# RWKV feature and scan stages: norms ahead of decays, key products on GpSimd, reciprocals right behind the masks

## Chip, cores and metric

The program runs on one core of a Trainium2 chip, in one launch. The metric is device microseconds of a whole execution, as the median of several runs.

## What is computed

One layer of a hybrid network. Its mixer has an RWKV-7 branch and an mLSTM branch, over 256 context tokens and then 512 latent tokens; a product-key expert block follows. The change touches the RWKV-7 branch alone:

```python
w_log = -softplus(-(w0 + einsum("btr,zrc->btzc", tanh(wd), w_up))) - 0.5
decay = exp(-exp(w_log))
a = sigmoid(a0 + einsum("btr,zrc->btzc", ad, a_up))
kk = k * k_k;  kk = kk / max(norm(kk, per head), 1e-12)
k_eff = k * (1 + (a - 1) * k_a)
# per head and direction, over time:
S = S * w_t - (S kk_t) (kk_t * a_t)^T + v_t k_t^T;   out_t = S r_t   # latent stream only
```

There are 8 heads of 64 channels and 2 directions (z = 0 and 1; z = 1 runs backwards in time). The context stream only hands its state on; the latent stream also gives outputs.

## The kernel before

Channels lie on partitions, tokens along the free dimension. 512 channels are 4 tiles of 128 (`PAIRS`, index c; two heads each). Phases follow each other, each a block of hand-written programs for the five engines that meet in semaphores; every engine runs its own list in order. The two touched phases run twice: `phase_rwkv_features` and `phase_rwkv_scan` for the context (tag `_c`, T = 256), then for the latents (tag `_x`, T = 512).

**Feature phase.** ScalarE takes `Tanh` of the decay input (L558), squares kk (L561) in one operation, and then goes through eight units n = (z, c). In each it takes the `Tanh` of the decay projection (`rw_th`, L567), an `Exp` into `w65` (L573, named w in the trace) and the `Tanh` of the rate projection into `qa` (L576). TensorE makes two projections a unit into four PSUM banks used in turn (L590, L592; a unit waits for the `qa` of the unit two before it), and behind all eight the four norm products of ones with the squares (L597), which take the same banks. VectorE scans each unit's decays into cumulative products `G` (L624; in the trace TENSOR_TENSOR_SCAN, in the listings below SCALAR_TENSOR_TENSOR), where the four scans of z = 1 wait until all eight `Exp` are there. It bounds the norms (L630); ScalarE takes `Ln` and `Exp` of them (L579, L581), each behind a table load; VectorE normalises `kk` (L633), and then makes, for each z over all four tiles: a = 0.5 tanh + 0.5 in `qa` (L637), the keys `ke` = k (1 - k_a + a k_a) in two steps (L639, L641) and the rates `qa` = a kk (L642). GpSimd does nothing here.

**Scan phase.** Chunks of `C` = 64 tokens, 4 for the context and 8 for the latents; two groups g, one a direction, in turn. GpSimd prepares a chunk (`prepare`): `pr` (kk by G, and r by G for the latents), then, once VectorE has `ginv` = 1/G (`inverse`, L957), `qs` = qa ginv and `ks` = ke ginv. TensorE multiplies `qs` and `ks` by `pr` (L880, marks Q and K): `pr` is `RW` = 3 C wide, its parts being the keys, the receptances (for the context a block of zeros), and a unit matrix. VectorE applies the masks to the products (`tm`, `td`, `bt`, `mt`, `at`), and five levels (`LEVELS`) of products and subtractions invert a triangular matrix (`ti`, `td` on VectorE, `xd` on ScalarE, the level masks `lm` on GpSimd, L757). Then R, U, O (latents) and S products, and VectorE updates the state `st` (L1001, L1003). The reciprocals for chunk i + 1 stand on VectorE behind the last level of chunk i, so `qs` and `ks` of chunk i + 1 come after that on GpSimd. TensorE starts a chunk's Q of group g when its `ks`, and the `st` of the chunk before, are done.

## Time and profile before

| | |
|---|---|
| median of 3 runs | 2789.89 us (2789.34 to 2801.12) |
| profiled execution | 2820.51 us, its span 2818.5 us |
| busy in the span: PE, DVE, ACT, POOL | 2583.1, 1331.7, 1026.9, 768.5 us |
| granted TensorE clock, mean | 0.94 |

The phases the change touches lie in this stretch of the same span, 458 us of it:

| stretch, us | what | PE busy | DVE | ACT | POOL | granted clock |
|---|---|---|---|---|---|---|
| 391.5 to 424.5 | context features | 12.89 | 18.93 | 16.34 | 0.00 | 0.55 |
| 424.5 to 546.5 | context scan, 4 chunks | 109.02 | 63.84 | 41.01 | 44.65 | 0.94 |
| 546.5 to 599.5 | latent features | 18.60 | 32.59 | 24.09 | 0.00 | 0.61 |
| 599.5 to 849.5 | latent scan, 8 chunks | 237.04 | 136.24 | 90.16 | 100.56 | 0.97 |

Phases meet in barriers, so a stretch ends when its last engine does. In a timeline row the columns are start, duration, engine, line and operation, output and inputs with shapes, count, and in brackets the idle time before it and who ended it. A row that merges several instructions gives the time from the first start to the last end. One fp32 matmul shows as two records.

### The profile page before, as it was taken

The numbers are of one execution on the slowest core, as the hardware profiler recorded it, in microseconds if no ns is written. First come the engines' busy times: TensorE is split into PE (matmuls) and PEld (weight loads), VectorE is DVE, ScalarE is ACT, GpSimd is POOL, SyncE is SP. The second block draws the span as 40 slices with busy tenths as digits, with TensorE's granted clock in tenths as the row PEclk, the third lists the DMA queues.
The fourth block names the chain that finished last, engine by engine and source line by source line (L and its number), as shares of the span: only waits on it lengthen the run. The fifth ranks groups of instructions, "written<-read, shape, count | busy, mean of one in ns | idle before, by whom it ended". The sixth has DMA issues, their size and how long they took to land. (4 is left out here: it accounts for less than half of the span.)

```text
span 2818.5 us, 53257 instructions
## 1 busy us (share of the span) xinstructions
PE 2583.1 (92%) x19772; PEld 2115.8 (75%) x19772; DVE 1331.7 (47%) x2679; ACT 1026.9 (36%) x1763; POOL 768.5 (27%) x627
## 2 busy tenths in 40 slices
PE   7999948849995898699999999999999999999998
PEld 3884527739993786588778888887888888888886
...
GB/s 251 192 149 37 0 0 2 2 1 0 0 1 95 89 97 52 121 127 69 122 122 173 216 174 170 168 194 216 145 134 220 192 195 189 198 187 200 184 203 60
DMA packets 163765, 348.58 MB, mean 124 GB/s; under 512 B 13352, under 2 KB 79400, under 8 KB 161648
## 3 DMA queue, kind: packets, MB, share of 16 engines
...
q8 instruction: 45, 0.74, 0.1%
...
## 5 line engine op out<-in xcount | busy, mean ns | idle before, releaser
L85 PE MATMUL ps_a<-h_hi,u_hi 128*128 128x512 f32 x1024 | 406.9, 397 | 14.1 <-issue 5.6
L2522 DVE TENSOR_TENSOR v_lo<-v_raw,v_hi 128x1024 fp32r<-128x1024 f32 x128 | 158.3, 1236 | 536.1 <-ACT v_hi L2480 536.1
L86 PE MATMUL ps_a<-h_hi,u_lo 128*128 128x512 f32 x1024 | 400.6, 391 | 0.0
L87 PE MATMUL ps_a<-h_lo,u_hi 128*128 128x512 f32 x1024 | 400.4, 391 | 0.0
L2480 ACT ACTIVATE v_hi<-v_raw 128x1024 fp32r<-128x1024 f32 x128 | 135.8, 1061 | 478.5 <-PE ps_a L87 470.2
L85 PE MATMUL ps_y<-gated_hi,v_hi 128*128 128x512 f32 x768 | 299.6, 390 | 3.1 <-DVE gated_lo L2524 3.1
L86 PE MATMUL ps_y<-gated_hi,v_lo 128*128 128x512 f32 x768 | 299.3, 390 | 0.0
L87 PE MATMUL ps_y<-gated_lo,v_hi 128*128 128x512 f32 x768 | 299.2, 390 | 0.0
L85 PEld LDWEIGHTS ps_a<-h_hi,u_hi 128*128 128x128 f32 x1024 | 193.8, 189 | 53.5 <-issue 14.2
L87 PEld LDWEIGHTS ps_a<-h_lo,u_hi 128*128 128x128 f32 x1024 | 193.3, 189 | 40.6
L86 PEld LDWEIGHTS ps_a<-h_hi,u_lo 128*128 128x128 f32 x1024 | 193.7, 189 | 37.9
L1876 ACT ACTIVATE act<-ps_a 128x512 f32<-128x512 f32 x128 | 76.4, 597 | 394.9 <-PE ps_a L87 383.8
L2332 POOL TENSOR_SCALAR mixed<-iota,w_token 128x128 f32<-128x128 f32 x128 | 149.5, 1168 | 213.3 <-PE ps_w L2351 197.7
L1860 POOL TENSOR_TENSOR u_lo<-u_raw,u_hi 128x1024 fp32r<-128x1024 f32 x64 | 155.5, 2434 | 175.4 <-ACT u_hi L1856 175.4
L1860 DVE TENSOR_TENSOR u_lo<-u_raw,u_hi 128x1024 fp32r<-128x1024 f32 x64 | 78.4, 1225 | 242.3 <-ACT u_hi L1856 242.3
L85 PEld LDWEIGHTS ps_y<-gated_hi,v_hi 128*128 128x128 f32 x768 | 144.6, 188 | 33.6 <-DVE v_lo L2522 3.5
L86 PEld LDWEIGHTS ps_y<-gated_hi,v_lo 128*128 128x128 f32 x768 | 144.6, 188 | 30.0
L87 PEld LDWEIGHTS ps_y<-gated_lo,v_hi 128*128 128x128 f32 x768 | 144.4, 188 | 30.1
L1856 ACT ACTIVATE u_hi<-u_raw 128x1024 fp32r<-128x1024 f32 x128 | 134.5, 1051 | 41.1 <-DMA u_raw<-in_uT 41.1
L1667 POOL TENSOR_TENSOR mg_w_lo<-mg_raw,mg_w_hi 128x1024 fp32r<-128x1024 f32 x36 | 87.7, 2436 | 197.8 <-ACT mg_w_hi L1716 197.8
L2383 ACT ACTIVATE w_block<-ps_w 128x512 f32 x128 | 141.3, 1104 | 0.0
L2351 PEld LDWEIGHTS ps_w<-mixed 128*128 128x128 f32 x1024 | 124.1, 191 | 5.0
...
## 6 DMA issues: line engine op xcount, KB each, us to landing
u_raw<-in_uT SPq DMA_DIRECT2D x128, 512.0 KB, 3.5
v_raw<-in_v SPq DMA_DIRECT2D x128, 512.0 KB, 4.8
a_scratch<-act SPq DMA_DIRECT2D x128, 256.0 KB, 2.2
w_scratch<-w_block SPq DMA_DIRECT2D x8, 4096.0 KB, 12.0
...
gated<-a_scratch SPq DMA_DIRECT2D x128, 256.0 KB, 4.8
...
```

The lines of the kernel that those rows point to most:

```text
L85: pe.matmul(out, wh, xh, start=first, stop=False)
L86: pe.matmul(out, wl, xh, start=False, stop=False)
L87: return pe.matmul(out, wh, xl, start=False, stop=last)
L1667: g.tensor_tensor(wl[:, k], raw[:, k], wh[:, k], ALU.subtract).then_inc(w_lo, 1)
L1856: act.activation(self.uh[:, q], self.raw[:, q % 2], ACT.Copy).then_inc(self.hi, 1)
L1860: eng.tensor_tensor(self.ul[:, q], self.raw[:, q % 2], self.uh[:, q], ALU.subtract).then_inc(self.lo, 1)
L1876: act.activation(self.act[:, q % 2], self.ps[q % 2][:], ACT.Gelu).then_inc(self.out, 1)
L2332: g_.tensor_scalar(oi[:, s, SUB - 1], iota, cur[:, s, 0:1], cur[:, s, 1:2], ALU.is_equal, ALU.mult).then_inc(built_p, 1)
L2351: m = pe.matmul(ps[s][:, k, :], oi[:, s, k], oj[:, s, k], start=True, stop=True)
L2383: act.activation(wb[:, half, :, bass.ds(g * BODY + dt, SUB)].rearrange("p j t -> p t j"), ps[s][:], ACT.Copy).then_inc(evac[s], 1)
L2480: act.activation(vh[:, q], v_raw[:, q], ACT.Copy).then_inc(v_hi, 1)
L2522: v.tensor_tensor(vl[:, q], v_raw[:, q], vh[:, q], ALU.subtract).then_inc(v_lo, 1)
```

## The change

In the feature phase the squares are made tile by tile ahead of the units; the norm products stand behind the second unit's projections and have PSUM banks of their own (`ps_rn`). ScalarE's order in a unit becomes decay `Tanh`, rate `Tanh`, `Exp`; its `Ln` and `Exp` for the norms stand between the units of z = 0 and z = 1. GpSimd makes the keys from tanh directly (a `tensor_scalar` and a `tensor_tensor` per unit). VectorE makes the rates with one `scalar_tensor_tensor` per unit, (tanh + 1) kk, which is twice the rate, and waits for the unit's `tensor_scalar` on GpSimd; the factor 0.5 goes into the masks and into `qt`. In the scan the context's `pr` loses its block of zeros (`RW` = 2 C), and the reciprocals for the next chunk stand right behind the masks. The diff leaves out unchanged parts and the two old loops over the units, on ScalarE and for the scans, which stand in the functions above.

```diff
@@ -520,12 +520,12 @@
             same = (r[:, None] // (2 * size)) == (r[None, :] // (2 * size))
             return same & ((r[:, None] // size) != (r[None, :] // size))
 
-        out[:, z, M_NEG1_ST] = -(off(1) & s_t).astype(np.float32)
+        out[:, z, M_NEG1_ST] = -0.5 * (off(1) & s_t).astype(np.float32)
         out[:, z, M_STRICT] = s_t
-        out[:, z, M_NEG_INCL] = -(s_t | np.eye(C, dtype=bool)).astype(np.float32)
+        out[:, z, M_NEG_INCL] = -0.5 * (s_t | np.eye(C, dtype=bool)).astype(np.float32)
         out[:, z, M_INCL] = s_t | np.eye(C, dtype=bool)
         for n, size in enumerate(LEVELS):
-            out[:, z, M_OFF + n] = off(size) & t_s
+            out[:, z, M_OFF + n] = 0.5 * (off(size) & t_s)
     return np.concatenate([out, out], 0)
 
@@ phase_rwkv_features @@
         half = sb("rw_half" + tag, [P, 4, PAIRS])
-        one_ka = sb("rw_1ka" + tag, [P, PAIRS])
+        ka = sb("rw_ka" + tag, [P, 2, PAIRS])
         w65 = sb("w65" + tag, [P, PAIRS, nch, C + 1])
         first = sb("w65_first" + tag, [P, nch, C + 1])
...
         ps = [ctx.enter_context(nc.psum_tensor(f"ps_rf{k}" + tag, [P, 512], F32)) for k in range(4)]
+        ps_n = [ctx.enter_context(nc.psum_tensor(f"ps_rn{k}" + tag, [P, 512], F32)) for k in range(PAIRS)]
...
         @block.scalar
         def _(act):
             act.activation(f[0:64, 12, :], f[0:64, 12, :], ACT.Tanh).then_inc(tanh_wd, 1)
+            for c in range(PAIRS):
+                act.wait_ge(sq_in, c + 1)
+                act.activation(tmp[:, c, :], b.kk[:, c, 0:T], ACT.Square).then_inc(sq_done, 1)
             act.wait_ge(half_done, 1)
-            act.wait_ge(sq_in, 1)
-            act.activation(tmp[:], b.kk[:, :, 0:T], ACT.Square).then_inc(sq_done, 1)
...
+            for n, (z, c) in enumerate(units):
+                act.wait_ge(proj, n + 1)
+                act.activation(th[:, n % 2], ps[2 * (n % 2)][:, 0:T], ACT.Tanh, bias=half[:, z, c:c + 1],
+                               scale=0.5).then_inc(th_done, 1)
+                act.activation(b.qa[:, z, c, 0:T], ps[2 * (n % 2) + 1][:, 0:T], ACT.Tanh,
+                               bias=half[:, 2 + z, c:c + 1], scale=0.5).then_inc(a_done, 1)
+                act.wait_ge(th_done, n + 1)
+                if z == 1:
+                    act.wait_ge(slot_done, 2)
+                act.activation(w65[:, c, :, 1:] if z == 0 else w65[:, c, :, 0:C],
+                               th[:, n % 2].rearrange("p (n t) -> p n t", t=C), ACT.Exp,
+                               bias=b.eps[:, 2:3], scale=-HALF_DECAY).then_inc(dec_done, 1)
+                if n == PAIRS - 1:
+                    act.wait_ge(norm_max, 1)
+                    act.activation(tmp[:], tmp[:], ACT.Ln).then_inc(norm_root, 1)
+                    act.wait_ge(norm_root, 1)
+                    act.activation(tmp[:], tmp[:], ACT.Exp, scale=-0.5).then_inc(norm_root, 1)
         @block.tensor
         def _(pe):
-            pe.wait_ge(tanh_wd, 1)
-            for n in range(2 * PAIRS):
-                z, c = n // PAIRS, n % PAIRS
+            def project(n):
+                z, c = units[n]
                 if n >= 2:
                     pe.wait_ge(a_done, n - 1)
                 pe.matmul(ps[2 * (n % 2)][:, 0:T], wa_up[0:64, z, c * P:(c + 1) * P], f[0:64, 12, :],
                           start=True, stop=True)
                 pe.matmul(ps[2 * (n % 2) + 1][:, 0:T], wa_up[64:P, z, c * P:(c + 1) * P], f[64:P, 12, :],
                           start=True, stop=True).then_inc(proj, 1)
-            pe.wait_ge(sq_done, 1)
-            pe.wait_ge(a_done, 2 * PAIRS)
+            pe.wait_ge(tanh_wd, 1)
+            for n in range(2):
+                project(n)
             for c in range(PAIRS):
-                mm = pe.matmul(ps[c][:, 0:T], b.block_ones[:], tmp[:, c, :], start=True, stop=True)
-            mm.then_inc(norm_mm, 1)
+                pe.wait_ge(sq_done, c + 1)
+                pe.matmul(ps_n[c][:, 0:T], b.block_ones[:], tmp[:, c, :], start=True, stop=True).then_inc(norm_mm, 1)
+            for n in range(2, len(units)):
+                project(n)
+        @block.gpsimd
+        def _(g):
+            g.wait_ge(half_done, 1)
+            for n, (z, c) in enumerate(units):
+                g.wait_ge(a_done, n + 1)
+                ke = b.ke[:, z, c, 0:T]
+                g.tensor_scalar(ke, b.qa[:, z, c, 0:T], ka[:, 0, c:c + 1], ka[:, 1, c:c + 1], ALU.mult,
+                                ALU.add).then_inc(pool, 1)
+                g.wait_ge(pool, 2 * n + 1)
+                g.tensor_tensor(ke, ke, f[:, 4 + c, :], ALU.mult).then_inc(pool, 1)
         @block.vector
         def _(v):
             link = Count(v, dve)
-            link(v.tensor_scalar(half[:], vecs[:, 0:4, :], 0.5, None, ALU.mult))
-            v.tensor_scalar(one_ka[:], vecs[:, 5, :], -1.0, 1.0, ALU.mult, ALU.add).then_inc(half_done, 1)
-            v.wait_ge(half_done, 1)
             for c in range(PAIRS):
-                m = v.tensor_scalar(b.kk[:, c, 0:T], f[:, 4 + c, :], vecs[:, 4, c:c + 1], None, ALU.mult)
-            m.then_inc(sq_in, 1)
+                v.tensor_scalar(b.kk[:, c, 0:T], f[:, 4 + c, :], vecs[:, 4, c:c + 1], None, ALU.mult).then_inc(sq_in, 1)
+            v.tensor_scalar(half[:], vecs[:, 0:4, :], 0.5, None, ALU.mult)
+            v.tensor_scalar(ka[:, 0], vecs[:, 5, :], 0.5, None, ALU.mult)
+            v.tensor_scalar(ka[:, 1], vecs[:, 5, :], -0.5, 1.0, ALU.mult, ALU.add).then_inc(half_done, 1)
             link(v.memset(first[:], 0.0))
             link(v.memset(first[:, :, 0:1], 1.0))
...
-            v.wait_ge(norm_mm, 1)
-            v.wait_ge(sq_done, 1)
+            v.memset(w65[:, :, :, 0:1], 0.0).then_inc(slot_done, 1)
+            def decay(n):
+                z, c = units[n]
+                v.wait_ge(dec_done, n + 1)
+                w = w65[:, c].rearrange("p n t -> p (n t)")
+                g = b.G[:, z, c, 0:nch * (C + 1)]
+                if z:
+                    w, g = w[:, ::-1], g[:, ::-1]
+                v.tensor_tensor_scan(out=g, data0=w, data1=first[:].rearrange("p n t -> p (n t)"), initial=0.0,
+                                     op0=ALU.mult, op1=ALU.add).then_inc(scanned, 1)
+            def rates(n):
+                z, c = units[n]
+                v.wait_ge(a_done, n + 1)
+                v.wait_ge(pool, 2 * n + 1)
+                qa = b.qa[:, z, c, 0:T]
+                v.scalar_tensor_tensor(out=qa, in0=qa, scalar=1.0, in1=b.kk[:, c, 0:T], op0=ALU.add,
+                                       op1=ALU.mult).then_inc(normed, 1)
+            v.wait_ge(slot_done, 1)
+            decay(0)
+            decay(1)
             for c in range(PAIRS):
-                m = v.tensor_scalar(tmp[:, c, :], ps[c][:, 0:T], 1e-24, None, ALU.max)
+                v.wait_ge(norm_mm, c + 1)
+                m = v.tensor_scalar(tmp[:, c, :], ps_n[c][:, 0:T], 1e-24, None, ALU.max)
             m.then_inc(norm_max, 1)
+            decay(2)
+            decay(3)
+            v.wait_ge(scanned, PAIRS)
+            v.memset(w65[:, :, :, C:C + 1], 0.0).then_inc(slot_done, 1)
             v.wait_ge(norm_root, 2)
             link(v.tensor_tensor(b.kk[:, :, 0:T], b.kk[:, :, 0:T], tmp[:], ALU.mult))
-            for z in range(2):
-                v.wait_ge(a_done, (z + 1) * PAIRS)
-                qa, ke = b.qa[:, z, :, 0:T], b.ke[:, z, :, 0:T]
-                link(v.tensor_scalar(qa, qa, 0.5, 0.5, ALU.mult, ALU.add))
-                for c in range(PAIRS):
-                    m = v.tensor_scalar(ke[:, c], qa[:, c], vecs[:, 5, c:c + 1], one_ka[:, c:c + 1], ALU.mult, ALU.add)
-                link(m)
-                link(v.tensor_tensor(ke, ke, f[:, 4:8, :], ALU.mult))
-                link(v.tensor_tensor(qa, qa, b.kk[:, :, 0:T], ALU.mult))
+            v.wait_ge(slot_done, 2)
+            for n in range(PAIRS):
+                rates(n)
+            for n in range(PAIRS, 2 * PAIRS):
+                decay(n)
+                rates(n)
@@ phase_rwkv_scan @@
-        RW = 3 * C
+        RW = (3 if need_out else 2) * C
+        UN = RW - C
...
-            if not need_out:
-                g_.wait_ge(state_in, 2)
...
-                act.activation(pr[g][:, :, 2 * C:], b.unit[:].unsqueeze(1).to_broadcast([P, PAIRS, C]),
+                act.activation(pr[g][:, :, UN:], b.unit[:].unsqueeze(1).to_broadcast([P, PAIRS, C]),
...
-                    act_s[g].mark(act.activation(quad(qt[g]), wide(g, 0, 2 * C), ACT.Copy, scale=-1.0))
+                    act_s[g].mark(act.activation(quad(qt[g]), wide(g, 0, UN), ACT.Copy, scale=-0.5))
...
-                    act_s[g].mark(act.activation(quad(kt[g]), wide(g, 1, 2 * C), ACT.Copy))
+                    act_s[g].mark(act.activation(quad(kt[g]), wide(g, 1, UN), ACT.Copy))
...
-                    v.memset(pr[g][:, :, C:2 * C], 0.0).then_inc(state_in, 1)
...
-            v.wait_ge(state_in, 2 if need_out else 4)
+            v.wait_ge(state_in, 2)
...
                     if need_out:
                         dve_s[g].mark(v.tensor_tensor(quad(at[g]), wide(g, 1, C), mask(g, M_INCL, four), ALU.mult))
+                if more:
+                    for g in range(2):
+                        inverse(i + 1, g)
...
                 turned(LEVELS[-1], 1)
-                if more:
-                    for g in range(2):
-                        inverse(i + 1, g)
                 for g in range(2):
```

How rows move. VectorE in the latent feature phase, from the last bound of the norms on; before:

```order
L630 TENSOR_SCALAR rw_tmp_x<-ps_rf3_x 128x512
L633 TENSOR_TENSOR kk<-kk,rw_tmp_x 128x2048
L637 TENSOR_SCALAR qa<-qa 128x2048
L639 TENSOR_SCALAR ke<-qa,rw_vecs,rw_1ka_x 128x512 x4
L641 TENSOR_TENSOR ke<-ke,fX 128x2048
L642 TENSOR_TENSOR qa<-qa,kk 128x2048
```

and with the change (`first` is the scan's second input):

```order
L652 TENSOR_SCALAR rw_tmp_x<-ps_rn3_x 128x512
L636 SCALAR_TENSOR_TENSOR G<-w65_x,w65_first_x 128x520 x2
L657 MEMSET w65_x 128x32
L659 TENSOR_TENSOR kk<-kk,rw_tmp_x 128x2048
L644 SCALAR_TENSOR_TENSOR qa<-qa,kk 128x512 x4
L636 SCALAR_TENSOR_TENSOR G<-w65_x,w65_first_x 128x520
L644 SCALAR_TENSOR_TENSOR qa<-qa,kk 128x512
L636 SCALAR_TENSOR_TENSOR G<-w65_x,w65_first_x 128x520
L644 SCALAR_TENSOR_TENSOR qa<-qa,kk 128x512
```

Three scan-and-rate pairs like the last follow. The operations over 2,048 columns for `qa` and `ke` are gone from VectorE, and each scan of z = 1 has a rate behind it. TensorE in the same phase, with the change, from the second unit's projections:

```order
L591 MATMUL ps_rf2_x<-fX,wa_up 128x512
L593 MATMUL ps_rf3_x<-fX,wa_up 128x512
L601 MATMUL ps_rn0_x<-rw_tmp_x,block_ones 128x512
L601 MATMUL ps_rn1_x<-rw_tmp_x,block_ones 128x512
L601 MATMUL ps_rn2_x<-rw_tmp_x,block_ones 128x512
L601 MATMUL ps_rn3_x<-rw_tmp_x,block_ones 128x512
L591 MATMUL ps_rf0_x<-fX,wa_up 128x512
L593 MATMUL ps_rf1_x<-fX,wa_up 128x512
```

The four norm products stood behind the sixteenth projection before, and now stand ahead of the fifth. VectorE in the latent scan's loop, behind `bt` of the second group; before:

```order
L73 REGISTER_ALU
L976 TENSOR_TENSOR mt0_x<-ps_rs01_x,rwkv_masks 128x256
L978 TENSOR_TENSOR at0_x<-ps_rs01_x,rwkv_masks 128x256
L976 TENSOR_TENSOR mt1_x<-ps_rs11_x,rwkv_masks 128x256
L978 TENSOR_TENSOR at1_x<-ps_rs11_x,rwkv_masks 128x256
L73 REGISTER_ALU
L981 TENSOR_TENSOR ti0_x<-ti0_x,ps_rs01_x 128x256
```

and with the change:

```order
L73 REGISTER_ALU
L997 TENSOR_TENSOR mt0_x<-ps_rs01_x,rwkv_masks 128x256
L999 TENSOR_TENSOR at0_x<-ps_rs01_x,rwkv_masks 128x256
L997 TENSOR_TENSOR mt1_x<-ps_rs11_x,rwkv_masks 128x256
L999 TENSOR_TENSOR at1_x<-ps_rs11_x,rwkv_masks 128x256
L77 ISA
L978 ISA
L978 RECIPROCAL ginv0_x<-G 128x256
L978 ISA
L978 RECIPROCAL ginv1_x<-G 128x256
L73 REGISTER_ALU
```

The two reciprocals, with their register instructions, now stand between the last mask and the first subtraction of the levels; they stood behind the last subtraction.

## Rows read from the trace of the kernel before

**Rows 1.** Windows, DVE, the latent feature stage: busy, count, PEclk, DMA share, GB/s

```profile
546.50:599.50 53.00, 32.59 (x38) 0.61 0.00 0
```

**Rows 2.** Timeline, context feature stage (start, us, engine, line, shapes); second: rw_th_c by tile

```profile
391.68 0.42 ACT L558 ACTIVATE fC<-fC 64x256 f32<-64x256 f32 x1 [1.25 <-PEq L105]
...
L567 ACT ACTIVATE rw_th_c<-ps_rf_c,rw_half_c x8: 456/464/474, 394.3 to 403.7; 128x256 f32<-128x256 f32 x8
...
412.50 1.06 ACT L581 ACTIVATE rw_tmp_c<-rw_tmp_c 128x1024 f32<-128x1024 f32 x1
...
422.92 1.22 DVE L642 TENSOR_TENSOR qa<-qa,kk 128x1024 f32<-128x1024 f32 x1
```

**Rows 3.** Latent feature stage: timeline; second and third by tile (min/median/max ns, starts)

```profile
546.82 0.63 ACT L558 ACTIVATE fX<-fX 64x512 f32<-64x512 f32 x1 [3.13 <-PEq L657]
...
L567 ACT ACTIVATE rw_th_x<-ps_rf_x,rw_half_x x8: 669/677/687, 550.8 to 564.6; 128x512 f32<-128x512 f32 x8
...
L597 PE MATMUL ps_rf_x<-rw_tmp_x,block_ones x8: 592/1061/1193, 566.8 to 572.5; 128*128 128x512 f32 x8
...
566.34 4.64 DVE L624 TENSOR_TENSOR_SCAN G<-w_x,w_first_x 128x520 f32<-128x520 f32 x4
...
577.55 1.28 ACT L581 ACT_TABLE_LOAD   x1
...
578.84 1.91 ACT L581 ACTIVATE rw_tmp_x<-rw_tmp_x 128x2048 f32<-128x2048 f32 x1
...
596.52 2.29 DVE L642 TENSOR_TENSOR qa<-qa,kk 128x2048 f32<-128x2048 f32 x1
```

**Rows 4.** What GpSimd takes: timeline of the context scan, then line L2332

```profile
437.72 6.20 POOL L757 TENSOR_TENSOR lm_c<-lt_c,rwkv_masks 128x256 f32<-128x256 f32 x9 [2.93 <-ACT lt_c L801]
...
L2332 POOL TENSOR_SCALAR mixed<-iota,w_token x128: 790/792/1598, 1431.1 to 1880.5; 128x128 f32<-128x128 f32 x128
```

**Rows 5.** Timeline: GpSimd and VectorE at once, in the front phase and the latent scan

```profile
58.74 14.25 POOL L251 COPY h_f<-mixed 128x512 f32<-128x512 f32 x4 [13.54 <-ACT h_f L308]
...
67.02 0.74 DVE L447 SCALAR_TENSOR_TENSOR h_lo<-mixed,mod,h_hi 128x512 fp32r<-128x512 f32 x1
...
672.33 0.72 POOL L757 TENSOR_TENSOR lm_x<-lt_x,rwkv_masks 128x256 f32<-128x256 f32 x1 [2.84 <-ACT lt_x L801]
...
672.38 0.96 DVE L971 TENSOR_TENSOR td_x<-tm_x,unit 128x256 f32<-128x256 f32 x1
```

**Rows 6.** Timeline, PE and DVE: context scan, first chunk, then start of the second

```profile
425.74 0.72 POOL L741 TENSOR_TENSOR pr_c<-kk,G 128x256 f32<-128x256 f32 x1 [42.01 <-DVE pr_c L946]
...
433.87 2.83 PE L880 MATMUL ps_rs_c<-pr_c,qs_c 64*64 64x192 f32 x16 [1.04 <-POOL ks_c L749]
...
457.25 3.36 DVE L957 RECIPROCAL ginv_c<-G 128x256 f32 x2
...
461.54 0.89 DVE L1003 TENSOR_TENSOR st_c<-tm_c,G 128x256 f32<-128x256 f32 x1 [0.15 <-DVE tm_c L1001]
...
462.67 1.52 PE L880 MATMUL ps_rs_c<-pr_c,qs_c 64*64 64x192 f32 x16 [0.82 <-DVE st_c L1003]
...
464.35 1.52 PE L880 MATMUL ps_rs_c<-pr_c,qs_c 64*64 64x192 f32 x16 [0.16 <-POOL ks_c L749]
...
468.27 0.66 PE L854 MATMUL ps_rs_c<-unit,td_c 64*64 64x64 f32 x16
```

**Rows 7.** Timeline, PE and DVE: a later chunk of the latent scan

```profile
669.06 2.82 PE L880 MATMUL ps_rs_x<-pr_x,qs_x 64*64 64x192 f32 x32
...
674.86 0.41 DVE L978 TENSOR_TENSOR at_x<-ps_rs_x,rwkv_masks 128x256 f32<-128x256 f32 x1
...
678.50 0.42 DVE L981 TENSOR_TENSOR ti_x<-ti_x,ps_rs_x 128x256 f32<-128x256 f32 x1 [3.23 <-PE ps_rs_x L847]
```

**Rows 8.** Timeline: a reciprocal beside a GpSimd product, start of the latent scan

```profile
604.75 1.75 DVE L957 RECIPROCAL ginv_x<-G 128x256 f32<-128x256 f32 x1 [1.96 <-POOLq L69]
...
605.00 0.72 POOL L741 TENSOR_TENSOR pr_x<-kk,G 128x256 f32<-128x256 f32 x1 [0.41 <-POOL ks_x L749]
```

More of the change, by code:

```diff
@@ L552, in phase_rwkv_features @@
                                                         sem("rwf_max"), sem("rwf_sqrt"))
-        dve, scanned = sem("rwf_dve"), sem("rwf_scanned")
+        dve, scanned, slot_done, normed, pool = (sem("rwf_dve"), sem("rwf_scanned"), sem("rwf_slot"), sem("rwf_normed"),
+                                                 sem("rwf_pool"))
         block = ctx.enter_context(nc.Block())
+        units = [(z, c) for z in range(2) for c in range(PAIRS)]
         @block.scalar
@@ L558, in _ @@
             act.activation(f[0:64, 12, :], f[0:64, 12, :], ACT.Tanh).then_inc(tanh_wd, 1)
+            for c in range(PAIRS):
+                act.wait_ge(sq_in, c + 1)
+                act.activation(tmp[:, c, :], b.kk[:, c, 0:T], ACT.Square).then_inc(sq_done, 1)
             act.wait_ge(half_done, 1)
-            act.wait_ge(sq_in, 1)
-            act.activation(tmp[:], b.kk[:, :, 0:T], ACT.Square).then_inc(sq_done, 1)
-            for z in range(2):
-                for c in range(PAIRS):
-                    n = z * PAIRS + c
-                    act.wait_ge(proj, n + 1)
-                    act.activation(th[:, n % 2], ps[2 * (n % 2)][:, 0:T], ACT.Tanh, bias=half[:, z, c:c + 1],
-                                   scale=0.5).then_inc(th_done, 1)
-                    act.wait_ge(th_done, n + 1)
-                    if z == 1:
-                        act.wait_ge(scanned, c + 1)
-                    act.activation(w65[:, c, :, 1:] if z == 0 else w65[:, c, :, 0:C],
-                                   th[:, n % 2].rearrange("p (n t) -> p n t", t=C), ACT.Exp,
-                                   bias=b.eps[:, 2:3], scale=-HALF_DECAY).then_inc(dec_done, 1)
-                    act.activation(b.qa[:, z, c, 0:T], ps[2 * (n % 2) + 1][:, 0:T], ACT.Tanh,
-                                   bias=half[:, 2 + z, c:c + 1], scale=0.5).then_inc(a_done, 1)
@@ L578, in _ @@
-            act.wait_ge(norm_max, 1)
-            act.activation(tmp[:], tmp[:], ACT.Ln).then_inc(norm_root, 1)
-            act.wait_ge(norm_root, 1)
-            act.activation(tmp[:], tmp[:], ACT.Exp, scale=-0.5).then_inc(norm_root, 1)
+            for n, (z, c) in enumerate(units):
[15 more added lines that the diff above has]
+                    act.activation(tmp[:], tmp[:], ACT.Exp, scale=-0.5).then_inc(norm_root, 1)
@@ L609, in _ @@
+            v.tensor_scalar(half[:], vecs[:, 0:4, :], 0.5, None, ALU.mult)
+            v.tensor_scalar(ka[:, 0], vecs[:, 5, :], 0.5, None, ALU.mult)
+            v.tensor_scalar(ka[:, 1], vecs[:, 5, :], -0.5, 1.0, ALU.mult, ALU.add).then_inc(half_done, 1)
             link(v.memset(first[:], 0.0))
             link(v.memset(first[:, :, 0:1], 1.0))
-            for z in range(2):
-                slot = 0 if z == 0 else C
-                if z == 1:
-                    v.wait_ge(scanned, PAIRS)
-                    v.wait_ge(dec_done, 2 * PAIRS)
-                link(v.memset(w65[:, :, :, slot:slot + 1], 0.0))
-                for c in range(PAIRS):
-                    v.wait_ge(dec_done, z * PAIRS + c + 1)
-                    w = w65[:, c].rearrange("p n t -> p (n t)")
-                    g = b.G[:, z, c, 0:nch * (C + 1)]
-                    if z:
-                        w, g = w[:, ::-1], g[:, ::-1]
-                    v.tensor_tensor_scan(out=g, data0=w, data1=first[:].rearrange("p n t -> p (n t)"), initial=0.0,
-                                         op0=ALU.mult, op1=ALU.add).then_inc(scanned, 1)
@@ L631, in _ @@
             m.then_inc(norm_max, 1)
+            decay(2)
+            decay(3)
+            v.wait_ge(scanned, PAIRS)
+            v.memset(w65[:, :, :, C:C + 1], 0.0).then_inc(slot_done, 1)
             v.wait_ge(norm_root, 2)
             link(v.tensor_tensor(b.kk[:, :, 0:T], b.kk[:, :, 0:T], tmp[:], ALU.mult))
-            for z in range(2):
-                v.wait_ge(a_done, (z + 1) * PAIRS)
-                qa, ke = b.qa[:, z, :, 0:T], b.ke[:, z, :, 0:T]
-                link(v.tensor_scalar(qa, qa, 0.5, 0.5, ALU.mult, ALU.add))
-                for c in range(PAIRS):
-                    m = v.tensor_scalar(ke[:, c], qa[:, c], vecs[:, 5, c:c + 1], one_ka[:, c:c + 1], ALU.mult, ALU.add)
-                link(m)
-                link(v.tensor_tensor(ke, ke, f[:, 4:8, :], ALU.mult))
-                link(v.tensor_tensor(qa, qa, b.kk[:, :, 0:T], ALU.mult))
+            v.wait_ge(slot_done, 2)
```

## The prediction

> **What bounds the kernel now.** I read the page's header first (PE busy 92% of the span, so only a stretch where PE waits can give much), then the windows by stage, then the timelines of the two feature phases and of chunk boundaries in the scans, then single operations that run on two engines at once.
>
> In the latent feature phase VectorE is busy 32.6 of 53 us and the granted clock is 0.61 [rows 1]. The phase is a serial chain: eight units on ScalarE, the scans of z = 1, the norm products, two table loads with `Ln` and `Exp`, then VectorE alone. It runs from 546.82 to 598.81, 52.0 us [rows 3]; the context's from 391.68 to 424.14, 32.5 us [rows 2]. In the scans PE is all but continuous, so there only PE's own work and the gaps at chunk boundaries count. In the context scan Q of the second chunk waits for `st`, stretched to 0.89 us, and for the last `ks`, which comes late because its reciprocal does [rows 6]. In the latent scan the 32 Q records of a later chunk run in 2.82 us with no wait [rows 7]: the O products give GpSimd time.
>
> **The feature phases.** All times are from the phase's start.
>
> Latents, up to the norms' `Exp`. A product of 512 columns costs PE about 1.65 us here (8 records, starts 566.8 to 572.5) [rows 3]. PE must now do two units' projections, four norm products and a third unit before ScalarE gets that unit: 0.8 + 7 x 1.65 = 12.3. ScalarE, whose third unit began near 8 before (first at 4.0, two more at 1.97), stands idle; this is the cost of the order. Two units at 1.9 (seven took 13.8) give 16.2, and two table loads with `Ln` and `Exp`, 2 x (1.28 + 1.91), end at 22.7 [rows 3]. Before, that `Exp` ended at 33.9. Another table load before the second four units isn't listed, as `Tanh` followed `Exp` without one.
>
> Latents, the rest. VectorE has `kk` (2.29), eight rates and four scans. A rate is taken as a `scalar_tensor_tensor` of 512 columns, 0.74 and some 0.66 back to back [rows 5]; the scans take 4.64 for four [rows 3]: 12.2 together. GpSimd has four units left, for the second four `qa` come only now. A product costs it 0.69 per 256 columns (6.20 for nine), so 1.4 for 512 [rows 4]. Its `tensor_scalar` of this width isn't in the trace: the nearest is 0.79 for 128 columns [rows 4], so it is 0.8 if that is all fixed cost, 3.2 if it is all columns; I take 1.4, as the product, which moves more. That is 11.1.
>
> Whether 12.2 and 11.1 overlap is the question. A VectorE addition with both inputs in SBUF took 0.96 beside a GpSimd product of 0.72, and four GpSimd copies took 14.25 while VectorE ran two-input operations back to back [rows 5]. They take turns, and all the VectorE work here has two SBUF inputs. Taking turns, with an estimated 0.6 for four handoffs: 22.7 + 12.2 + 11.1 + 0.6 = 46.6, a gain of **5.4**.
>
> The Trainium skill (SBUF — State Buffer, Who interferes with whom) says the same as a rule: a VectorE instruction with two SBUF inputs and a GpSimd one that reads SBUF exclude each other for a whole instruction. By that rule the scans, which no row shows beside GpSimd, count too; the sum above stands. The Trainium skill (GPSIMD Engine Reference, Engine selection and Performance versus the Vector engine) speaks against moving the keys at all: elementwise work belongs on VectorE, GpSimd being about twice as slow with two inputs, though near line rate with one (769 ns for 512 columns at best). By that figure the phase would end some 2.5 us earlier than my sum; the trace has only the 128-column row.
>
> Context, the same at half the width: 0.6 + 7 x 0.85 = 6.5; two units 2.5 (seven took 9.4) [rows 2]; 2 x (1.28 + 1.06) = 4.7; so 13.7. Then 1.2 + 8 x 0.38 + 4 x 0.6 = 6.6 on VectorE, 4 x (1.0 + 0.7) = 6.8 on GpSimd (the 1.0 between 0.8 and 1.6 from the same row), 0.6: 27.8 against 32.5, **4.7**.
>
> **The context scan.** `pr` has 128 columns instead of 192. Sixteen records take 1.52 at 192 columns and 0.66 at 64 [rows 6], so 64 columns fewer save 0.43, and there are four such groups a chunk: 1.7. At the boundary GpSimd's `qs`, `ks` and `pr` now lie in the middle of the chunk, beside operations with one PSUM input. `st` falls from 0.89 to about 0.42, and Q of the second group starts behind the first (464.35 against 462.67 + 1.31) but for its own `st`: 0.6 together. Three such chunks: 3 x 2.3 = 6.9. In the first chunk PE is slow (2.83 for 16) [rows 6]; the three groups behind the last `ks` save 0.87 each at that pace, but the pace rises at about the same moment as before, so I take 1.2 (bounds 0.9 and 2.6). The memsets of `pr` no longer hold GpSimd's start at 425.74: 0.7. Sum **8.8**, bounds 7.5 and 10.5.
>
> **The latent scan.** No width changes, and the boundary shows no wait to win. The two reciprocals (3.36) [rows 6] go where VectorE idles 3.23 before the first level subtraction [rows 7]: 0.13 late a chunk. With the context's three and the latents' seven chunks that is at most 1.3, less what PE has in hand; I take **-0.5**. The end of a chunk gains nothing from their leaving, since the state update waits for S.
>
> At nothing: squares by tile (ScalarE waits for the first projections meanwhile; without that cover their three extra start-ups, under 1 us), the 0.5 in masks and `qt` (same instructions), the memset of the slot behind the scans (ScalarE has its `Ln` to do meanwhile).
>
> **Sum.** 5.4 + 4.7 + 8.8 - 0.5 = 18.4 us. The profiled execution would go from 2820.5 to 2802.1. It stands 30.6 us above the median, and no stretch here depends on what slowed it, so the same 18.4 comes off the median: 2789.9 - 18.4 = **2771.5 us**. A measurement tells about 0.5% (14 us) from no change.
>
> **Rivals.**
> - *The engines do not take turns at the scans and rates.* The latent phase ends at 22.7 + 12.2 + one last product 1.4 = 36.3, gain 15.7; the context's at 13.7 + 6.6 + 0.7 = 21.0, gain 11.5. With 8.3 from the scans: 35.5 us, 2754; about 2751 if PE also reaches the higher clock early, since it has no pause now. Against it: the 0.96 row. For it: the scan may be limited by its own recurrence. 14%.
> - *GpSimd's `tensor_scalar` is dear*, 3.2 and 1.6. Rates wait for it, so it is in the chain: 4 x 1.8 = 7.2 longer, and the first four units (4 x 4.6, and 4.6 of scans between) are through only some 4.4 late. The latent phase ends at 58.2, 6.2 worse than before; the context's at 27.8 + 2.4 + 1.5 = 31.7, 0.8 better. Total gain 2.9: 2787. For it: the row's 6.2 ns a column. Against it: that row is a comparison of few columns. 14%.
> - *Slower: GpSimd's masks shut out the reciprocals.* Behind the masks on VectorE GpSimd runs nine products in 6.20 without a break [rows 4]. If a reciprocal had to wait for them, the level subtractions, and with them PE, would be some 5 us late in each of 10 chunks: 50 - 18 = 32 us slower, 2822. It undoes the gain from 1.9 us a chunk. Against it: a reciprocal that had a GpSimd product of 0.72 wholly inside it took 1.75, no more than half of 3.36 and its start-up [rows 8]. 5%.
> - *The narrower products cost PE the same*, being held by weight loads: 6.4 less, 12.0, 2778. Against it: 64 columns are much cheaper than 192. 7%.
> - The forecast: 60%.
>
> **How the numbers follow.** Within the forecast the unknown costs (`tensor_scalar` from 0.8 to 2 us, the clock in the feature phases) give 2764 to 2779, of which about 0.49 in 0.60 lies beyond 14 us. Faster by over 0.5%: 0.49 + 0.14 + 0.03 = 0.66; slower by over 0.5%: the third rival and a stray measurement, 0.06; within: 0.28. The range 2753 to 2787 takes in the first two rivals' times nearly, and leaves out the slower one.
>
> **What would show it.** Latent feature phase 46.6 us and context 27.8, with GpSimd and VectorE alternating in the last 20; the norms' `Exp` ending at 22.7 and 13.7. ScalarE idle some 4 us before its third unit. Context chunks 2.3 us shorter each; latent chunks as long as before, to 0.1. `ks` of the next chunk done before the third level. A feature phase of 36 us, or of 58, or latent chunks 5 us longer, would each name its rival.

## The result, and the profile after

| | before | after |
|---|---|---|
| median of the runs (us) | 2789.6 | 2754.5 |
| lowest (us) | 2788.1 | 2750.8 |
| profiled execution (us), its span | 2820.5, 2818.5 | 2750.8, 2749.0 |

The change is faster: the ratio is 0.985, 95% interval 0.981 to 0.990. That is some 41 us (29 to 54), where the medians alone differ by 35.1. The time lies in the forecast's range (2753 to 2787), but the gain is about twice the 18.4 us of the sum.

The head of the page, after. TensorE's busy time fell with the narrower products and with more of the span at the higher clock; GpSimd gained 32 operations, VectorE has 12 fewer.

```profile
span 2749.0 us, 53275 instructions
PE 2534.6 (92%) x19772; PEld 2091.0 (76%) x19772; DVE 1318.8 (48%) x2667; ACT 1025.4 (37%) x1769; POOL 814.1 (30%) x659
```

The windows of the four stages, after (context features, context scan, latent features, latent scan; busy us of each engine, granted clock, DMA share, GB/s); the second row answers to the context scan of before, the third to [rows 1].

```profile
363.06:385.73 22.67, 9.53 (x40) 5.44 (x40) 15.55 (x32) 15.65 (x33) 14.27 (x16) 0.65 0.00 0
385.73:498.75 113.02, 100.76 (x2944) 97.70 (x2944) 61.27 (x124) 40.64 (x114) 44.84 (x64) 0.95 0.01 2
498.75:536.10 37.35, 15.29 (x40) 4.79 (x40) 28.87 (x33) 23.47 (x34) 27.14 (x16) 0.66 0.00 0
536.10:781.20 245.10, 232.56 (x6656) 226.80 (x6657) 135.37 (x274) 89.92 (x259) 100.63 (x144) 0.98 0.00 1
```

The two spans differ by 69.5 us, and 28.6 of that isn't the change's: it lies ahead of the context features, which start at 363.06 instead of 391.68. Over all the profiles below that start lies between 361 and 392, at 364.4 in a kernel with the feature phase of before (1) and at 391.6 in one with the change's (8). In this pair the clock was granted at half speed for 60 us before, and mostly in full after (the same window of both kernels, before first):

```profile
280.00:340.00 60.00, 60.00 (x177) 28.56 (x178) 15.51 (x37) 13.41 (x46) 0.00 (x0) 0.50 0.00 0
```
```profile
280.00:340.00 60.00, 51.52 (x276) 29.41 (x276) 25.21 (x74) 28.42 (x105) 0.00 (x0) 0.83 0.00 1
```

So I compare stages, not totals. A feature phase runs here from ScalarE's first `Tanh` to GpSimd's first `pr` of the scan behind it, the scan from there to the start of the next stage. "st" is VectorE's update of the state at the end of a chunk. "kk" is the distance from the phase's start to VectorE's first operation behind the norms' `Exp`; "tail" is the rest of the phase. All from the timelines of the profiled executions, in us:

| kernel | context features (kk + tail) | context scan | first to last state update | latent features (kk + tail) | latent scan, to its first update |
|---|---|---|---|---|---|
| before | 34.1 (21.9 + 12.1) | 121.1 | 84.3 | 53.2 (34.0 + 19.2) | 249.1, 37.5 |
| after | 22.9 (13.0 + 9.9) | 112.8 | 76.9 | 37.4 (19.2 + 18.2) | 245.0, 34.6 |
| 1 scan part only | 33.5 | 111.8 | 76.2 | 51.6 | 248.5, 38.0 |
| 2 features only | 23.5 (12.8 + 10.7) | 119.1 | 84.8 | 37.4 (19.2 + 18.2) | 245.7, 35.2 |
| 3 keys on VectorE | 24.8 (14.0 + 10.8) | 112.7 | 76.7 | 37.0 (19.2 + 17.8) | 247.5, 37.8 |
| 4 norms behind | 21.4 (16.8 + 4.6) | 112.9 | 76.7 | 35.7 (27.4 + 8.3) | 247.3, 36.2 |
| 5 no keys | 20.9 (14.0 + 6.9) | 113.1 | 77.5 | 33.7 (21.4 + 12.3) | 248.4, 37.5 |
| 6 warm | 32.7 | 107.2 | 74.8 | 49.6 | 300.4, 37.8 |
| 7 rates in two | 26.5 (14.0 + 12.5) | 113.5 | 77.5 | 39.4 (17.5 + 21.9) | 248.5, 37.8 |
| 8 reciprocals behind | 23.9 (14.0 + 9.9) | 117.2 | 81.1 | 37.4 (19.2 + 18.2) | 245.6, 34.6 |
| 9 before, early | 28.9 (23.6 + 5.3) | 119.2 | 84.5 | 43.3 (35.6 + 7.7) | 248.0, 37.5 |
| 10 roots behind | 23.5 (18.9 + 4.6) | 113.6 | 77.0 | 35.9 (27.2 + 8.7) | 249.2, 38.7 |
| 11 the same, VectorE | 23.4 (18.9 + 4.6) | 114.2 | 77.0 | 34.5 (26.8 + 7.8) | 244.8, 34.3 |
| 12 the change again | 23.3 (13.4 + 9.9) | 112.8 | 77.2 | 37.4 (19.2 + 18.2) | 248.3, 37.6 |

The change took 27.0 us out of the feature phases, 8.2 out of the context scan and 4.1 out of the latent scan: 39.3 of the profiled pair.

The tail of the latent features, after (VectorE and GpSimd; start, duration). It answers to [rows 3] from `kk` on:

```profile
517.93 2.29 DVE L659 TENSOR_TENSOR kk<-kk,rw_tmp_x 128x2048 f32<-128x2048 f32 x1 [4.55 <-ACT rw_tmp_x L583]
519.15 1.71 POOL L611 TENSOR_SCALAR ke<-qa,rw_ka_x 128x512 f32<-128x512 f32 x1 [4.03 <-ACT qa L570]
520.25 4.02 DVE L644 SCALAR_TENSOR_TENSOR qa<-qa,kk 128x512 f32<-128x512 f32 x4
...
529.17 1.57 POOL L614 TENSOR_TENSOR ke<-ke,fX 128x512 f32<-128x512 f32 x1
529.55 2.29 DVE L636 TENSOR_TENSOR_SCAN G<-w_x,w_first_x 128x520 f32<-128x520 f32 x1
530.73 2.19 POOL L611 TENSOR_SCALAR ke<-qa,rw_ka_x 128x512 f32<-128x512 f32 x1
531.77 0.68 DVE L644 SCALAR_TENSOR_TENSOR qa<-qa,kk 128x512 f32<-128x512 f32 x1
532.37 1.64 DVE L636 TENSOR_TENSOR_SCAN G<-w_x,w_first_x 128x520 f32<-128x520 f32 x1
533.01 2.06 POOL L614 TENSOR_TENSOR ke<-ke,fX 128x512 f32<-128x512 f32 x1
```

Neither engine pauses, and the same operation takes now 1.64, now 2.29 us: they are in each other's way. The boundary of the first two context chunks, after, answers to [rows 6]; Q no longer comes in two pieces, 32 records with `st` at 0.43:

```profile
420.84 0.43 DVE L1025 TENSOR_TENSOR st_c<-tm_c,G 128x256 f32<-128x256 f32 x1 [0.15 <-DVE tm_c L1023]
421.51 1.96 PE L902 MATMUL ps_rs_c<-pr_c,qs_c 64*64 64x128 f32 x32 [0.35 <-DVE st_c L1025]
423.27 1.94 PE L902 MATMUL ps_rs_c<-pr_c,ks_c 64*64 64x128 f32 x32
```

In the latent chunks the first level subtraction starts as the second reciprocal ends, the place of [rows 7], and chunks stay 29.18 us apart (before 637.52 to 666.71, after 599.92 to 629.10):

```profile
579.18 3.35 DVE L978 RECIPROCAL ginv_x<-G 128x256 f32 x2
582.50 0.42 DVE L1006 TENSOR_TENSOR ti_x<-ti_x,ps_rs_x 128x256 f32<-128x256 f32 x1
```

### The profile page after: what moved, and what is told of

Read it like the earlier page. It is cut to its first block, busy times and chain, and to the rows that moved or that the text cites. A ratio compares the mean times of both kernels' runs of the same rounds, so it can differ in the third digit from the quotient of the medians.

```text
span 2749.0 us, 53275 instructions
## 1 busy us (share of the span) xinstructions
PE 2534.6 (92%) x19772; PEld 2091.0 (76%) x19772; DVE 1318.8 (48%) x2667; ACT 1025.4 (37%) x1769; POOL 814.1 (30%) x659
## 4 chain that ended last, share of the span: by engine, by line
PE 49%; DMA 1%; SPq 0%; ACT 0%; DVE 0%; issue 0%; ACTq 0%; DVEq 0%
PE ps_a L85 9%; PE ps_a L87 8%; PE ps_a L86 8%; PE ps_y L85 6%; PE ps_y L86 6%; PE ps_y L87 6%; PE ps_w L2373 4%; DMA w_scratch<-w_block 0%; DMA a_scratch<-act 0%; PE ps_y L2593 0%; DVE mixed L2554 0%; SPq L2457 0%; SPq L2462 0%; ACT L2526 0%; SPq L2452 0%
## 5 line engine op out<-in xcount | busy, mean ns | idle before, releaser
L85 PE MATMUL ps_a<-h_hi,u_hi 128*128 128x512 f32 x1024 | 407.5, 398 | 12.3 <-issue 5.6
L85 PEld LDWEIGHTS ps_y<-gated_hi,v_hi 128*128 128x128 f32 x768 | 144.5, 188 | 33.5 <-DVE v_lo L2544 3.5
```

Source lines behind the costliest of these rows:

```text
L85: pe.matmul(out, wh, xh, start=first, stop=False)
```

## The experiments

The theory: the engines do take turns, but the sum had the parts too dear. The rival among the prediction's own: no turns are taken, since its 36.3 and 21.0 us for the two phases are close to what came. Totals of one kernel scatter by 10 to 40 us, so the stage table above decides; a ratio is to the kernel before, whose medians beside the experiments were 2798 to 2804 us.

**1 and 2: the two halves.** 1 is the kernel before with `RW`, `UN`, the memsets and the place of `inverse` as in the change; 2 the change with the scan of before.

> The kernel before with the change's scan part alone (128 columns instead of 192 in the context scan, no memsets of pr, reciprocals behind the masks; factors as before). In the changed kernel's trace the context scan is 9.1 us shorter and the latent scan 4.0, of which 2.9 lie in its first chunk. Theory (the first latent chunk is shorter only because TensorE gets its higher clock sooner after the shorter feature phase): context scan -9 us, latent scan 0 within 1 us, feature phases unchanged at 33.05 and 53.2 us; 9 us in all, about 2780.6 against 2789.6. Rival (the moved reciprocals shorten the latent chunks too): latent scan -3 or more, 12 to 13 us in all, about 2777.

> The changed kernel with the scan of before (192 columns, memsets, reciprocals behind the levels; the halved factors stay, since the new features need them). Theory: context feature phase 22.7 us, latent 37.3 us (26.2 less than before), first latent chunk 2.9 shorter by the clock, context chunks back at 27.1 us: 29 us in all, about 2760.5 against 2789.6. Rival (reciprocals are what shortened the first latent chunk): 26 us in all, about 2763.5, and 37.5 us from the start of the latent scan to its first state update instead of 34.6.

Measured: 0.997 (0.993 to 1.001) and 0.991 (0.988 to 0.995). The scan part takes 9.2 us off the context scan; in the latents first to last update is 209.3 us, as in the change. The feature part gives 10.5 and 15.8 us. The halves add up. The first latent chunk took 38.0 in 1 and 35.2 in 2, as the theory had it, but see 12.

**3: keys back on VectorE.**
```diff
-            for n, (z, c) in enumerate(units):   # GpSimd
...
-                g.tensor_scalar(ke, b.qa[:, z, c, 0:T], ...)
...
-                g.tensor_tensor(ke, ke, f[:, 4 + c, :], ALU.mult)
+            def key(n):                          # VectorE, behind each decay(n)
...
+                link(v.tensor_scalar(ke, b.qa[:, z, c, 0:T], ...))
+                v.tensor_tensor(ke, ke, f[:, 4 + c, :], ALU.mult).then_inc(pool, 1)
```


> The changed kernel with the keys back on VectorE, unit by unit, GpSimd idle in the feature phases. Theory (GpSimd and VectorE take turns, and GpSimd needs 2.05 us for a unit of 512 columns where VectorE needs 1.31): behind the norms' Exp VectorE has kk 2.29, eight rates 5.3, four scans 4.64 and four keys 5.2, so 17.4 in place of the 17.7 that the two engines took together: latent phase 37 within 1 us, context 22.7 within 1, the time the same as the changed kernel's, about 2752 to 2755. Rival (the two engines overlap): VectorE's four keys come on top, latent phase 42.5, context 25.4, 8 us slower than the changed kernel.

Measured: 0.987 (0.982 to 0.992), latents 37.0, context 24.8 (its `kk` came 1.0 later than in the change, with the clock; the tail is 1.0 longer). Four more units of keys on VectorE, and the latent tail is 0.4 shorter. Undisturbed, the operations are short (VectorE's timeline of this kernel, latents):

```profile
535.46 1.23 DVE L625 TENSOR_TENSOR_SCAN G<-w_x,w_first_x 128x520 f32<-128x520 f32 x1
536.61 0.52 DVE L632 TENSOR_SCALAR ke<-qa,rw_ka_x 128x512 f32<-128x512 f32 x1
537.17 0.69 DVE L633 TENSOR_TENSOR ke<-ke,fX 128x512 f32<-128x512 f32 x1
537.97 0.69 DVE L640 SCALAR_TENSOR_TENSOR qa<-qa,kk 128x512 f32<-128x512 f32 x1
```

**4: norms behind.** The norm products, maxima, `Ln` and `Exp` come behind all eight units.
```diff
-                if n == PAIRS - 1:
+                if n == 2 * PAIRS - 1:
                     act.wait_ge(norm_max, 1)
```


> The changed kernel with its norm products, Ln and Exp behind all eight units again, keys on GpSimd and one-operation rates kept. Theory (the order brings little, since GpSimd then has its keys done by the time of the norms): latents 2.6 + 8 x 1.9 + norm products and maxima 5 + tables, Ln, Exp 6.4 + kk 2.3 + eight rates 5.3 = 36.8 against 37.3, context 23.5 against 22.7: same time within 1 us. Rival (norms ahead of the second four units is what hides the chain): latents 43 or more, context 26, 9 us slower.

Measured: 0.987 (0.981 to 0.993), latents 35.7, context 21.4, 1.7 and 1.5 shorter than in the change: its first named part, the norms ahead, brings nothing in this company. (TensorE ran the products of this latent phase at the higher clock, which can account for the 1.7: in 6 and 7, which have the change's order and the higher clock up to that point, `kk` comes at 17.5 instead of 19.2.) GpSimd's last units lie under `Ln` and `Exp`, with VectorE idle, and give the prices that the prediction lacked (GpSimd's timeline of this kernel):

```profile
518.34 1.27 POOL L614 TENSOR_TENSOR ke<-ke,fX 128x512 f32<-128x512 f32 x1
519.60 0.77 POOL L611 TENSOR_SCALAR ke<-qa,rw_ka_x 128x512 f32<-128x512 f32 x1
```

**5: no keys.** The two operations and the wait on them are left out.

> The changed kernel without the keys (GpSimd sets ke to a constant at the start of each feature phase; the output is not the reference's). It measures what VectorE alone needs. Theory (turns are taken): behind the norms' Exp 2.29 + 8 x 0.66 + 4 x 1.16 = 12.2, so the latent phase ends at 32 us instead of 37.3 and the context's at 20 instead of 22.8; scans 1.16 and rates 0.66 each. Rival (VectorE is as long without GpSimd): 36 to 37 us, scans 1.6 to 2.3.

Measured (one execution): the latent tail falls from 18.2 to 12.3, the context's from 9.9 to 6.9. `kk` came 2.2 us later than in the change, so the phase is 33.7 and not 32: the norm products began 0.7 later, behind the filling of `ke`, and took 5.7 us instead of 4.2 at the lower clock. VectorE alone (its timeline in this kernel, latents):

```profile
531.44 2.50 DVE L636 SCALAR_TENSOR_TENSOR qa<-qa,kk 128x512 f32<-128x512 f32 x4
533.85 1.23 DVE L629 TENSOR_TENSOR_SCAN G<-w_x,w_first_x 128x520 f32<-128x520 f32 x1
```

Four rates in 2.50 where the change has 4.02, scans at 1.23 where it has up to 2.29. With 3 this fells "no turns": GpSimd's four units, 8.1 us by themselves (4 x (0.77 + 1.26)), cost the tail 5.9.

The filling itself, one `memset` on GpSimd, shows the turns at their plainest. VectorE's four one-input products beside it took 4.93 us, where the change, with GpSimd idle, has 1.67; the first of them alone took 3.75 and ended 0.3 us after the `memset` (GpSimd, then VectorE; then VectorE in the change):

```profile
507.71 3.51 POOL L607 MEMSET ke<- 128x4096 f32 x1 [19.43 <-POOLq L672]
507.75 4.93 DVE L613 TENSOR_SCALAR kk<-fX,rw_vecs 128x512 f32<-128x512 f32 x4 [0.32 <-PEq L672]
```
```profile
498.78 1.67 DVE L620 TENSOR_SCALAR kk<-fX,rw_vecs 128x512 f32<-128x512 f32 x4 [0.32 <-PEq L680]
```

**6: warm.** Sixteen unread products at the end of each phase, four behind each scan from the fourth to the seventh, and eight (context) or four (latents) ahead of the first Q.

> The changed kernel with products that nobody reads on the idle TensorE: four beside each z = 1 scan at the end of the feature phases, and a few ahead of the first Q in each scan. Theory (the first chunk is long because TensorE starts it at the lower clock, and that only because it idled before): granted clock 1.0 from the first Q on, the first latent chunk 34.6 -> about 32, the first context chunk 34.4 -> about 32, feature phases as before, 5 us faster than the changed kernel. Rival (the clock in the first chunk is set by something else, or the products only delay Q): 0 to 3 us slower.

Measured: 1.011 (1.006 to 1.015), far worse than the rival. The two kinds of filler behaved differently. Those at the end of the latent features, 64 rows deep, kept TensorE busy for 25 us and held the phase up; the clock was at the higher level when they began, fell to the half 2.6 us later and stayed there. Those ahead of the first Q, 128 rows deep, began at half speed and had the higher clock within 3.6 us, before the first Q, in both streams (TensorE's timeline of this kernel, first two rows latents, last two context; then two windows of the latents, TensorE's busy time and granted clock):

```profile
537.95 25.09 PE L609 MATMUL ps_rn_x<-fX,wa_up 64*128 64x512 f32 x32 [1.50 <-issue]
564.15 5.51 PE L898 MATMUL ps_rs_x<-kk,block_ones 128*128 128x512 f32 x8 [1.12 <-ACT pr_x L807]
...
407.33 5.43 PE L898 MATMUL ps_rs_c<-kk,block_ones 128*128 128x256 f32 x16 [1.12 <-ACT pr_c L807]
412.69 1.09 PE L910 MATMUL ps_rs_c<-pr_c,qs_c 64*64 64x128 f32 x16
```
```profile
542.00:563.00 21.00, 21.00 (x25) 0.50 0.00 0
567.90:569.60 1.70, 1.70 (x6) 1.00 0.00 0
```

So the theory is right for the context: with the higher clock at the first Q its first chunk fell from 34.4 to 30.8 us. The latents' did not get shorter: Q began 1.1 us later in the scan, and TensorE waited 2.0 us in the chunk for nothing that the profile shows.

Such waits then fill the loop, though nothing in it had changed: each of the six steps from one update to the next inside it took 37.7 to 39.3 us instead of 29.2. The last chunk, which is written out behind the loop, took its usual time (30.3, in the change 30.8). In five chunks TensorE waited 17.8 us ahead of Q (first fence, its waits from 600 to 760: total, times, longest), the clock fell to the half for some 3.4 us each time, so that 32 records of Q took 4.50 us where they take 2.82 at the higher clock (second), and the queue that carries instructions moved 100 packets in the run instead of 45 (third, the page's queues: packets, MB, share); 39 of them came in these 160 us, and none in the matching stretch of the change (572.6 to 732.6):

```profile
PE ps_rs_x L910 <- issue: 17.8, 5, 3.8
```
```profile
608.43 4.50 PE L910 MATMUL ps_rs_x<-pr_x,qs_x 64*64 64x192 f32 x32 [3.65 <-issue]
```
```profile
q8 instruction: 100, 1.64, 0.3%
```

**7: rates in two.** `add` one, then times `kk`.

> The changed kernel with each rate in two VectorE operations (add one, then times kk), as before. The one-input operation of 512 columns is about 0.40 by the row of 0.69 for 1024. Theory (VectorE's work in the tail adds up with GpSimd's): latents +3.3 us (40.6), context +2 (24.8), 5 us slower. Rival (GpSimd sets the tail, being busy without a break in it, and a one-input operation runs beside it): 1 us or less slower.

Measured: 0.996 (0.992 to 1.001). The tails are 3.7 and 2.6 longer, near the theory. The one-input operation is stretched beside GpSimd as well, 1.49 against 0.40 once GpSimd is done (VectorE's timeline of this kernel):

```profile
537.65 1.49 DVE L644 TENSOR_SCALAR qa<-qa 128x512 f32<-128x512 f32 x1
...
547.23 0.40 DVE L644 TENSOR_SCALAR qa<-qa 128x512 f32<-128x512 f32 x1
```

**8: reciprocals behind.** Only the call of `inverse` is moved back.

> The changed kernel with the reciprocals behind the levels again. Theory (narrow products give 1.7 of the 2.5 us a context chunk, the reciprocals the rest; latents indifferent): context from first to last state update 76.9 -> 79.3, latents 209.3 within 0.7. Rival (without O products the narrower products bring nothing unless ks is early): 76.9 -> 82 or more.

Measured (one execution): 81.1, between theory and rival; the latents' 209.8 is within the theory's 0.7. Narrow products alone give 1.1 a chunk (84.3 to 81.1 over three), because Q's halves then wait for `st` and for the late `ks`; the early reciprocals give 1.4. TensorE's timeline of this kernel at a boundary:

```profile
477.53 1.09 PE L902 MATMUL ps_rs_c<-pr_c,qs_c 64*64 64x128 f32 x16 [0.73 <-DVE st_c L1024]
479.21 1.09 PE L902 MATMUL ps_rs_c<-pr_c,qs_c 64*64 64x128 f32 x16 [0.59 <-POOL ks_c L773]
```

**9: the kernel before with its work moved forward.**
```diff
+            def unit_ops(z, c):        # VectorE: behind each z = 0 scan; z = 1 behind the maxima
...
+                link(v.tensor_scalar(qa, qa, 0.5, 0.5, ALU.mult, ALU.add))
+                link(v.tensor_scalar(ke, qa, vecs[:, 5, c:c + 1], one_ka[:, c:c + 1], ALU.mult, ALU.add))
+                link(v.tensor_tensor(ke, ke, f[:, 4 + c, :], ALU.mult))
```


> The kernel before with one thing moved: of the work behind the norms, the halving of the rates and the keys of each unit run on VectorE as soon as that unit is there (z = 0 behind each scan, z = 1 behind the maxima, while ScalarE does Ln and Exp). No GpSimd, no one-operation rates, scan as before. Theory (what shortened the feature phases is that this work leaves the end of the chain, whichever engine does it): behind the norms' Exp only kk 2.3 and two products of 2.29 are left, latents 53.2 -> 42, context 33.5 -> 26.5, 18 us of the change's 26 in the feature phases. Rival (GpSimd's share is what counts): 5 us or less in all.

Measured: 0.992 (0.989 to 0.996); 9.9 us off the latents, 5.1 off the context. More than half of the 27.0 comes from this alone, without GpSimd and with no operation fewer. It fell 3 us short of the theory: the four z = 1 units outlast `Ln` and `Exp`, so that `kk` now waits for VectorE's own keys, 1.8 us in the latents (`Exp` ended at 573.4). The last key and the tail of the latents, VectorE's timeline of this kernel:

```profile
574.47 0.69 DVE L617 TENSOR_TENSOR ke<-ke,fX 128x512 f32<-128x512 f32 x1
575.20 2.29 DVE L645 TENSOR_TENSOR kk<-kk,rw_tmp_x 128x2048 f32<-128x2048 f32 x1
577.52 4.62 DVE L648 TENSOR_TENSOR qa<-qa,kk 128x2048 f32<-128x2048 f32 x2
```

**10 and 11: looking for a better one.** 10: norm products where the change has them, `Ln` and `Exp` behind the last unit. 11: the same with the keys on VectorE.

> The changed kernel with Ln and Exp behind the last unit, the norm products staying where the change has them; keys on GpSimd. Theory: third unit at 9.0, six units to 20.4, tables, Ln and Exp to 26.8, kk and eight rates 2.5 + 4.9 with GpSimd already done: latents 34.5 to 35 against 37.3, context 21.5 against 22.8: 3 to 4 us faster than the changed kernel. Rival (Ln and Exp between the two halves are hidden work): latents 40 or more.

> The kernel of the run on the roots, with the keys on VectorE instead of GpSimd (z = 1 ones in the time of Ln and Exp). Theory (turns; all keys fit in VectorE's idle time, four of them, 5.0 us, in the 6.4 of Ln and Exp): the same as that run within 0.7 us a phase, latents 34.5, context 21.5. Rival (VectorE becomes the bound): latents 37 or more.

Measured: 0.989 (0.982 to 0.995) and 0.988 (0.982 to 0.994). Latents 35.9 and 34.5 against 37.4, context no better (23.5 and 23.4 against 22.9 and 23.3). Three us at most, which these totals don't show: neither is shown to beat the change, nor is 4. VectorE has all four z = 1 keys through before `kk`, without GpSimd (VectorE's timeline of 11):

```profile
535.68 0.69 DVE L633 TENSOR_TENSOR ke<-ke,fX 128x512 f32<-128x512 f32 x1
536.85 2.29 DVE L664 TENSOR_TENSOR kk<-kk,rw_tmp_x 128x2048 f32<-128x2048 f32 x1 [0.48 <-ACT rw_tmp_x L583]
539.18 4.91 DVE L640 SCALAR_TENSOR_TENSOR qa<-qa,kk 128x512 f32<-128x512 f32 x8
```

**12: the change again.**

> The changed kernel itself, for comparison on the same chip: latents 37.3, context 22.8 to 23.9, the state updates of the context 76.9 apart from first to last, 209.3 for the latents; the first latent chunk 34.6 if it belongs to the change, or 37.5 in this execution if it falls one way or the other with the clock.

Measured: 0.984 (0.979 to 0.990). Every stage repeats to 0.5 us but one: the first latent chunk took 37.6 instead of 34.6. The clock rose 7.3 us after the first Q here and 3.4 us after it in the first profile; the second Q shows it, at the lower clock here and at the higher there (12, then after):

```profile
546.99 2.82 PE L902 MATMUL ps_rs_x<-pr_x,qs_x 64*64 64x192 f32 x16 [1.23 <-POOL ks_x L773]
```
```profile
545.15 1.52 PE L902 MATMUL ps_rs_x<-pr_x,qs_x 64*64 64x192 f32 x16 [1.23 <-POOL ks_x L773]
```

TensorE had been idle for 18.2 us before the first Q in both, and the kernel is the same, so these 3 us aren't a sure gain of the change. All profiles but 6's fall into two groups: where the clock rose some 3 us after the first latent Q (after, 2, 4, 8, 11) the chunk took 34.3 to 36.2 us, where it rose 7 to 9.5 us after it, 37.5 to 38.7. The three kernels with the feature phase of before (before, 1, 9) are all in the second group; whether a shorter phase makes the first likelier isn't shown.

## Why the prediction was wrong

Its mechanisms held in the main; three terms of its sum for the feature phases were too large. By its own ends the latent phase took 36.9 us (498.75 to 535.61) where it said 46.6, the context's 22.3 where it said 27.8.

- **The norms' `Exp` at 22.7: it ended at 19.2.** The step priced all seven products ahead of ScalarE's third unit at the slow 1.65. Here the granted clock was 1.0 in most of that part: the four norm products, with no pause ahead of them, took 4.20 us together (0.59 for most records), so the third unit began at 9.1 instead of 12.3, and what follows it was as forecast. 3.5 us; in the context 0.7. This size is not fixed: with all these products at the higher clock `kk` came at 17.5 (6, 7). After, TensorE, then ScalarE's third unit and the norms' `Exp`:

```profile
502.51 4.20 PE L601 MATMUL ps_rn_x<-rw_tmp_x,block_ones 128*128 128x512 f32 x8
507.81 0.69 ACT L568 ACTIVATE rw_th_x<-ps_rf_x,rw_half_x 128x512 f32<-128x512 f32 x1 [2.80 <-PE ps_rf_x L593]
...
515.99 1.91 ACT L583 ACTIVATE rw_tmp_x<-rw_tmp_x 128x2048 f32<-128x2048 f32 x1
```

- **GpSimd 11.1: it needs 8.1.** The `tensor_scalar` of 512 columns is 0.77, not 1.4: the lower bound of [rows 4] was the right end, and the product is 1.26, not 1.4. 3 us; in the context 4 x (0.56 + 0.72) = 5.1 for 6.8.
- **12.2 + 11.1 + 0.6, strictly one after the other.** The turns are real (3, 5), scans and one-input operations included, but a GpSimd operation costs VectorE less than its length: 5.9 us for 8.1, and no handoff on top. With VectorE's own 11.8 for 12.2 this is 3.2 us. The three together are the 9.7. The rule cited from the Trainium skill (SBUF — State Buffer, Who interferes with whom) agrees for the scans and for the one-input operations of 5 and 7, which by that page can take the shared port too. That one side waits "for the whole instruction" is what the `memset` of 5 shows; the tail shows less, for its two engines need 11.8 and 8.1 us by themselves, 19.9 in all, and took 17.7.
- **The context scan, 8.8: 9.1** (424.73 to 546.82 before, 385.73 to 498.75 after; these ends take in the memsets of `pr`, those of the table don't), right. Its parts were less so: 1.1 a chunk for the width and 1.4 for the boundary, for 1.7 and 0.6 (8). A wait took the place of the columns until the reciprocals moved.
- **The latent scan, -0.5: 0** in the repeated chunks, for what the first chunk gained is the clock's (12). The reciprocals fit exactly.
- **The rival "no turns"** had 36.3, 21.0 and 2754 us, against 36.9, 22.3 and 2754.5, for a reason that 3 and 5 disprove. That its number came out is luck: in the latents its `Exp` came 3.5 us too late and its tail was 4.1 too short.
- "Slower by the masks", "narrow products cost the same" and "`tensor_scalar` dear" did not come. That the profiled execution's excess of 30.6 us was elsewhere fits: its context features begin 28.6 us later than in the profile after.

9.7 + 5.5 + 0.3 + 0.5 above the forecast's 18.4 are 34.4; the medians differ by 35.1. With an interval of 29 to 54 us on the total, the stages carry this account and not the near match.
